# Down products one pass later and gathers indexed three passes ahead in the expert loop of a hybrid attention and MoE block

## The reference

```python
def _swiglu(x, wg, wu, wd):
    return (jax.nn.silu(x @ wg) * (x @ wu)) @ wd

def _moe(h, w_r, b_r, wg, wu, wd, swg, swu, swd):
    idx, wts = _route(h, w_r, b_r)
    return _moe_routed(h, idx, wts, wg, wu, wd) + _swiglu(h, swg, swu, swd)
```

## Time and profile before

| | |
|---|---|
| median of 3 runs | 3259.84 us |
| profiled execution, span | 3254.0 us; its own time about the median: 5.84 us lie around the span |
| expert loop of layer 0, first gate/up to last down products | 918.3 to 1796.6 us, 64 passes |
| expert loop of layer 1 | 2519.3 to 3213.1 us, 48 passes |
| TensorE busy, whole span | 2721.8 us (84%) |
| gate/up matmuls (L1402) | 806.1 us busy |
| down matmuls (L1414) | 417.5 us busy |

### The profile page before, as it was taken

The page is one execution under the profiler, slowest core; times in us unless marked ns, Lnnn a source line. Parts: engine busy times, 40 slices in busy tenths (PEclk is TensorE's granted clock), DMA queues, the critical chain, the costliest instruction groups (busy, mean ns, idle before and its releaser), DMA issues. The chain is left out here.

```text
span 3254.0 us, 44151 instructions
## 1 busy us (share of the span) xinstructions
PE 2721.8 (84%) x12983; PEld 1458.1 (45%) x12984; DVE 1251.3 (38%) x3394; ACT 562.2 (17%) x1256; POOL 1085.5 (33%) x948
## 2 busy tenths in 40 slices
PE   6688988996969999999989368899977888889884
PEld 5364755654533333333333146666743333333331
DVE  5653553433323333333333564453533323323223
ACT  2121321311001111111111212321310111111111
POOL 0675798901011111111111273767410111111111
PEclk9898999997989999999999689899987999999997
DMA  6120212114187998999896411122134999998983
GB/s 225 33 75 26 87 56 93 49 40 161 58 314 228 330 303 262 298 304 300 293 333 212 166 33 55 33 85 89 53 109 172 339 391 370 386 386 261 367 331 110
DMA packets 193069, 635.88 MB, mean 195 GB/s; under 512 B 18768, under 2 KB 113232, under 8 KB 159440
## 3 DMA queue, kind: packets, MB, share of 16 engines
q1 hardware_dynamic: 159856, 530.30, 43.4%
q0 software_dynamic: 33120, 104.37, 14.0%
HBM read 577.72 MB, written 76.94 MB: 201 GB/s over the span
## 5 line engine op out<-in xcount | busy, mean ns | idle before, releaser
L1402 PE MATMUL ps<-wgu,xT 128*64 128x512 f32 x3584 | 806.1, 602 | 82.9 <-issue 65.4
L1402 PEld LDWEIGHTS ps<-wgu,xT 128*64 128x64 f32 x3584 | 297.7, 138 | 588.9 <-issue 588.9
L1342 POOL DMA_INDIRECT X<-h_rows,gix x116 | 119.0, 1026 | 1070.5 <-DVE wc L1520 1024.9
L1414 PE MATMUL ps<-wd,hiddenT 128*64 128x512 f32 x1792 | 417.5, 605 | 37.1 <-issue 35.5
L544 PE MATMUL ps<-w_in,hT 128*128 128x512 f32 (+3 forms) x1152 | 395.6, 504 | 16.2 <-DMA wup_1B<-in_w_up 4.4
L544 PEld LDWEIGHTS ps<-w_in,hT 128*128 128x128 f32 x1152 | 212.4, 202 | 184.7 <-issue 177.0
L1361 POOL DMA_INDIRECT ffn_rows<-Y,six x112 | 179.0, 1598 | 252.2 <-issue 221.6
L1414 PEld LDWEIGHTS ps<-wd,hiddenT 128*64 128x64 f32 x1792 | 148.3, 139 | 234.8 <-issue 227.5
L1530 DVE TENSOR_TENSOR hidden<-silu,ps 128x256 f32<-128x256 f32 x112 | 47.2, 421 | 395.0 <-ACT silu L1477 395.0
L1389 PE MATMUL ps<-cst,X 128*128 128x128 f32 x912 | 147.3, 286 | 56.0 <-DMA X<-h_rows,gix 55.4
L1477 ACT ACTIVATE silu<-ps 128x256 f32<-128x256 f32 x112 | 42.9, 383 | 807.8 <-PE ps L1402 807.8
(11 more groups left out here) (453 smaller groups left out, 3716.0 us busy)
## 6 DMA issues: line engine op xcount, KB each, us to landing
wgu<-in_exp_gu SPq DMA_DIRECT2D x128, 2048.0 KB, 11.9
wd<-in_exp_d SPq DMA_DIRECT2D x128, 1024.0 KB, 10.3
ada_start<-in_ada_w SPq DMA_DIRECT2D x8, 1024.0 KB, 9.9
w_in<-in_w_in SPq DMA_DIRECT2D x4, 2048.0 KB, 8.2
w_in<-in_w_out SPq DMA_DIRECT2D x4, 2048.0 KB, 11.2
aw_0A<-in_ada_w SPq DMA_DIRECT2D x12, 512.0 KB, 4.0
aw_0B<-in_ada_w SPq DMA_DIRECT2D x12, 512.0 KB, 3.8
w_in<-in_w_in SPq DMA_DIRECT2D x2, 3072.0 KB, 10.7
```

What stands on the lines that cost most here:

```text
L1342: pool.indirect_dma_start(out=X[j][:, :], out_offset=None, in_=v.h2_dram, in_offset=bass.IndirectOffsetOnAxis(ap=gix[j][:, 0:1], axis=0), ...
L1402: last = pe.matmul(ps[h * HB:(h + 1) * HB, 0, :], xT[:, k, h * HB:(h + 1) * HB], wgu[w[h]][:, k, :], start=(k == 0), stop=(k == KD - 1))
L1414: last = pe.matmul(ps[h * HB:(h + 1) * HB, 1 + c, :], G[:, f, h * HB:(h + 1) * HB], wd[w[h]][:, f, c * 512:(c + 1) * 512], start=(f == 0), ...
```

## The change: what it does

In the changed code, TensorE's pass i turns all eight blocks of pass i + 1, then does the down products of pass **i - 1**, turns the hidden rows of pass i, makes the list of pass i + 3, and does the gate/up products of pass **i + 1** at its end. Gate/up of pass 0 stands before the loop, the down products of the last pass behind it; in pass 0 down products are done on zeros. It reads six table entries at its start: three of pass i - 1 and three of pass i + 1. The other engines follow: Y of pass i - 1 is written in pass i, gathers fetch pass i + 3 after the scatter, lists and marks are three ahead, the row numbers are kept in a tile of one column per pass. SyncE loads gate/up of expert e, then down of expert e - 1.

```diff
...
+                with sp.Fori(0, E // NB - 2) as group:
                     for w in range(NB):
-                        e = group * NB + w
-                        free = sp.value_load(table[0:1, bass.ds(e + T_FREE, 1)], min_val=0, max_val=pairs)
-
-                        sp.wait_ge(gate_up, free + GU_CREDIT)
-                        sp.dma_start(wgu[w][:, :, :].rearrange("p k n -> p (k n)"),
-                                     v.t["exp_gu"][l][bass.ds(e, 1)].rearrange("a p n -> (a p) n")).then_inc(w_gu[w], 16)
-                        sp.wait_ge(down, free + DOWN_CREDIT)
-                        sp.dma_start(wd[w][:, :, :].rearrange("p k n -> p (k n)"),
-                                     v.t["exp_d"][l][bass.ds(e, 1)].rearrange("a p n -> (a p) n")).then_inc(w_d[w], 16)
+                        e = group * NB + (NB + 1 + w)
+                        load_gate_up((w + 1) % NB, e, free_after(e))
+                        load_down(w, e - 1, free_after(e - 1))
...
-                def body(i, turn, j):
-                    pool.wait_ge(index, i + 3)
-                    pool.wait_ge(turned_b, i + 1)
-                    pool.wait_ge(wcol, i * 2 + 2)
-                    waited()
-                    gather(j)
+                def scatter(j):
+                    pool.sem_inc(y_free, 1)
+                    pool.indirect_dma_start(out=v.acc_dram, out_offset=bass.IndirectOffsetOnAxis(ap=six[j][:, 0:1], axis=0),
+                                            in_=Y[j][:, :], in_offset=None, compute_op=ALU.add).then_inc(added, 16)
+
+                def body(i, j):
+                    before = 1 - j
                     pool.wait_ge(y_act, i + (1 + CREDIT))
                     pool.wait_ge(y_dve, i + (1 + CREDIT))
                     pool.wait_ge(y_index, i + 1)
                     pool.wait_ge(added, i * 16 + 16)
-                    pool.sem_inc(y_free, 1)
-                    pool.indirect_dma_start(out=v.acc_dram, out_offset=bass.IndirectOffsetOnAxis(ap=six[j][:, 0:1], axis=0),
-                                            in_=Y[j][:, :], in_offset=None, compute_op=ALU.add).then_inc(added, 16)
-
+                    scatter(before)
+                    pool.wait_ge(index, i + (AHEAD + 1))
+                    pool.wait_ge(turned_b, i + 2)
+                    pool.wait_ge(wcol, i * 2 + 6)
+                    waited()
+                    gather(before)
...
+                def turn_rows(j):
+                    for k in range(KD):
+                        last = pe.transpose(ps[:, 3 + k // 4, k % 4 * P:(k % 4 + 1) * P], X[j][:, k * P:(k + 1) * P], v.ident)
+                        if k == 3:
+                            last.then_inc(turned_a, 1)
+                    last.then_inc(turned_b, 1)
...
-                def body(i, turn, odd):
-                    variant = entry(pe, T_VAR, i, 2 * NB - 1)
-                    landed = [entry(pe, T_LAND0 + h * TABN, i, E // NB * 16) for h in range(2)]
-                    pe.wait_ge(x_act, i + 1)
-                    pe.wait_ge(x_dve, i + 1)
-                    pe.wait_ge(hidden, i + CREDIT)
-                    by_buffers(variant, gate_up_products, landed, 0, 2 * NB)
-                    pe.wait_ge(index, i + 2)
-                    token_list(i + 2)
+                def entries(i):
+                    return entry(pe, T_VAR, i, 2 * NB - 1), [entry(pe, T_LAND0 + h * TABN, i, E // NB * 16) for h in range(2)]
+
+                def body(i, turn, odd, turns16):
+                    was, was_landed = entries(i - 1)
+                    now, now_landed = entries(i + 1)
                     with pe.If(odd < 1):
                         pe.wait_ge(gathered[1], turn * 16 + 16)
-                        turn_rows(1, 0)
+                        turn_rows(1)
                     with pe.Else():
                         pe.wait_ge(gathered[0], turn * 16 + 32)
-                        turn_rows(0, 0)
+                        turn_rows(0)
+                    pe.wait_ge(g_act, i + CREDIT)
+                    pe.wait_ge(g_dve, i + CREDIT)
+                    pe.wait_ge(y_act, i + CREDIT)
+                    pe.wait_ge(y_dve, i + CREDIT)
+                    by_buffers(was, down_products, was_landed, 0, 2 * NB)
                     pe.wait_ge(hidden, i + (1 + CREDIT))
                     turn_hidden()
-                    with pe.If(odd < 1):
-                        turn_rows(1, 1)
-                    with pe.Else():
-                        turn_rows(0, 1)
-                    pe.wait_ge(y_act, i + CREDIT)
-                    pe.wait_ge(y_dve, i + CREDIT)
-                    by_buffers(variant, down_products, [*landed, i + 1], 0, 2 * NB)
-
-                token_list(0)
-                pe.wait_ge(index, 1)
-                token_list(1)
+                    pe.wait_ge(index, i + AHEAD)
+                    pe.wait_ge(listed, i + (AHEAD + 1))
+                    token_list()
+                    with pe.If(i * 8 + 8 < turns16):
+                        pe.wait_ge(x_act, i + 2)
+                        pe.wait_ge(x_dve, i + 2)
+                        by_buffers(now, gate_up_products, now_landed, 0, 2 * NB)
+
+                for b in range(AHEAD):
+                    if b:
+                        pe.wait_ge(index, b)
+                    pe.wait_ge(listed, b + 1)
+                    token_list()
                 pe.wait_ge(gathered[0], 16)
-                turn_rows(0, 0)
-                turn_rows(0, 1)
+                turn_rows(0)
                 total = pe.value_load(table[0:1, T_COUNT:T_COUNT + 1], min_val=0, max_val=pairs)
+                turns16 = passes16(pe)
+                first, landed = entries(0)
+                pe.wait_ge(hidden, CREDIT)
+                pe.wait_ge(x_act, 1)
+                pe.wait_ge(x_dve, 1)
+                by_buffers(first, gate_up_products, landed, 0, 2)
                 with pe.Fori(0, -(-turns // STRETCH)) as stretch:
                     with pe.If(stretch * (STRETCH * U) < total):
                         with pe.Fori(0, STRETCH) as k:
                             turn = pe.snap(stretch * STRETCH + k)
                             with pe.If(turn * U < total):
                                 with pe.Fori(0, U) as odd:
-                                    body(pe.snap(turn * U + odd), turn, odd)
+                                    body(pe.snap(turn * U + odd), turn, odd, turns16)
+                last, landed = entries(turns16 // 8 - 1)
+                pe.wait_ge(g_act, turns16 // 8 + CREDIT)
+                pe.wait_ge(g_dve, turns16 // 8 + CREDIT)
+                pe.wait_ge(y_act, turns16 // 8 + CREDIT)
+                pe.wait_ge(y_dve, turns16 // 8 + CREDIT)
+                by_buffers(last, down_products, landed, 0, 2 * NB)
 
+                def row_index(i, j):
+
+                    dve.wait_ge(y_free, i + 1)
+                    dve.tensor_scalar(six[j][:, :], rows[:, bass.ds(i, 1)], cst[:, C_ADD:C_ADD + 1], None, ALU.add).then_inc(y_index, 1)
+
+                def y_half(i, j):
+
+                    dve.wait_ge(down, i + 1)
+                    dve.wait_ge(wcol, i * 2 + 2)
+                    dve.tensor_scalar(Y[j][:, 512:D], ps[:, 2, :], wc[j][:, 0:1], None, ALU.mult).then_inc(y_dve, 1)
+
+                def body(i, j):
+                    before = 1 - j
+                    e1, e3 = entries(i + 1), entries(i + AHEAD)
                     dve.wait_ge(silu, i + 1)
                     dve.tensor_tensor(HID[:, :], SG[:, :], ps[:, 0, FD:2 * FD], ALU.mult).then_inc(hidden, 1)
+                    x_half(i + 1)
+                    dve.wait_ge(indexed, i + AHEAD)
+                    mark_slots(i + AHEAD, e3, i * 4 + (4 * AHEAD + 2))
+                    row_index(i, before)
+                    y_half(i, before)
                     dve.wait_ge(g_turned, i + 1)
-                    dve.wait_ge(down, i + DOWN_CREDIT)
                     dve.tensor_copy(G[:, 1, :], ps[:, 7, 0:P]).then_inc(g_dve, 1)
-                    x_half(i + 1)
-                    dve.wait_ge(y_free, i + 1)
-                    dve.tensor_scalar(six[j][:, :], gix[j][:, :], cst[:, C_HALF:C_HALF + 1], None, ALU.add).then_inc(y_index, 1)
-                    dve.wait_ge(y_index, i + 1)
-                    dve.wait_ge(gathered[j], turn * 16 + 16)
-                    dve.wait_ge(indexed, i + 3)
-                    make_index(j, i * 4 + 11)
-                    dve.wait_ge(y_act, i + CREDIT)
-                    dve.wait_ge(y_dve, i + CREDIT)
-                    weight_column(e1, (j + 1) % U)
-                    dve.wait_ge(down, i + (1 + DOWN_CREDIT))
-                    dve.wait_ge(wcol, i * 2 + 2)
-                    dve.tensor_scalar(Y[j][:, 512:D], ps[:, 2, :], wc[j][:, 0:1], None, ALU.mult).then_inc(y_dve, 1)
-
...
```

More of the change, by code:

```diff
@@ L1300, in experts @@
         mark = sb("mark", [P, nt, P], F16)
-        itmp = sb("itmp", [P, 3])
+        itmp = sb("itmp", [P, 2])
+        rows = sb("rows", [P, TABN])
```

(50 more changed lines are left out.)

80 lines of the change are left out of this document (49 added, 31 removed).

## The result

The changed kernel takes 3455.19 us (median of 4 runs, 3451.25 to 3458.4) against 3259.84: 1.0603 times the time before, 95% interval 1.0589 to 1.0617. I had forecast 3297, and a range up to 3325. The profiled execution has a span of 3456.4 us against 3254.0, so +202.4 (more than the 195 between the medians, since the profiled execution of after is one of its two longer ones).

| stretch | before | after | more | forecast |
|---|---|---|---|---|
| from the first to the second gate/up | 15.2 / 15.2 | 18.5 / 19.1 | 7.2 | 0 |
| layer 0, 62 passes | 850.2 | 979.8 | 129.6 | 14 |
| layer 1, 46 passes | 665.7 | 694.9 | 29.2 | 3 |
| last gate/up to the end of the last down products | 12.9 / 12.9 | 29.0 / 23.7 | 26.9 | 21 |
| all outside the loops | | | 9.4 | 0 |

A forecast was written before the change was run, and what follows sets the result against it. Transfers and TensorE were both taken as bounds, with "issue" the largest single idle item in layer 0. Layer 0 +14, layer 1 +3 and ends +21 gave +38 on the 3259.84 us median: 3297 us, range 3242 to 3325.

The forecast's parts named there:

- my first rival: TensorE's queue covers the whole gate/up, so the 1.38 us idle a pass vanish: 3182 us; 5%.
- six entries 5 x 0.76 + 0.65 = 4.45: Sequencer behind the gate/up products: six table reads take 4.45 us of a 5.25 or 5.9 us walk.
- 0.09 for clock falls as before: Layer 0 pass: clock falls add 0.09 us, unchanged, to 13.81, giving 13.90 against 13.71.
- The 13.9 us pass: Sign in the profile after: a layer 0 pass takes 13.9 us.
- Transposes to down products, 0.13: Between the eight transposes and the down products, 0.13 us a pass of sequencer work stays uncovered.
- Down to gate/up 0: From down products through hidden transposes and list to gate/up: no idle time, or up to 0.3 us if it slips.
- Gathers' waits end: Gathers are issued 18 us ahead of use instead of 9.3, so their waits end in both layers.
- Layer 1, +3: Layer 1's loop: no gain because DMA engines are full over more than half; +3 us, bounds -18 and +20.
- Ends, +21: Last down products, moved behind each loop's exit, start late: +11.7 and +9.2 us, together +21, bounds 8 and 28.
- the seam is shorter: Sequencer's walk overlaps what was added in a row, 0.5 us a pass less: 3256 or 3246 us; 15%.
- the list comes late: VectorE's marks slip beyond the 0.3 us in hand, TensorE waits each pass: +34 us, 3331 us; 9%.
- SP starves layer 1: SP's new order starts loads 6 us later and empties DMA queues, 15 to 20 us: 3315 us; 11%.

The follow-up runs named there:

- late_reads: Changed kernel with the three table entries for the gate/up products read behind the down products, not behind the gate/up products; 3197.86 us, 0.9812 of before.
- packed: Changed kernel with variant and both landed counts in one table word, so TensorE reads 2 words a pass instead of 6; 3176.71 us, 0.9745 of before.
- before_six: Kernel before the change, with three more table entries read and not used at the start of each TensorE pass; 3584.14 us, 1.0995 of before.
- small_write: Changed kernel with the scatter replaced by a plain write of 16 columns of Y to fixed rows (layer 1 works on other data); 3290.85 us, 1.0107 of before.
- filled: Changed kernel with one useless 64x384 matmul behind each of the six table reads and the waits for Y ahead of them; 3528.93 us, 1.0813 of before.
- gather_first: Changed kernel with GpSimd issuing the gather ahead of the scatter in each pass; 3446.39 us, 1.0558 of before.
- plain_write: Changed kernel with the scatter replaced by a plain write of the whole of Y to fixed rows (layer 1 works on other data); 3356.88 us, one run.
- packed_late_scatter: Changed kernel with one packed table word per entry set (2 reads a pass) and layer 0's scatter issued behind those reads; 3255.81 us, 0.9977 of before.
- packed_plus2: Changed kernel with packed table words and two more unused table reads at each pass's start, 4 in all; 3267.56 us, 1.0027 of before.

## Why the prediction was wrong

- *The mechanism held.* The sequencer's walk behind the gate/up products sets the seam; late_reads and packed show it by taking it away, before_six by lengthening the old one. In the timeline's first pass the loop's ALU_OP stands at 1149.14, 2.88 us behind gate/up's start, so the cover from there is 4.21 us (I had 4.24), and the walk from there to the transposes at 1156.23 is 7.09: my 5.9 and 1.19 by which one read is held. The Trainium skill (TensorE: Matmul & The Clock Gate, the table at its head) gives the queue a depth of 64. If all 64 records of a gate/up stood in it, the cover would be the whole 7.09, as in my first rival; the runs disagree again, with the sequencer held for 2.6 us at the full clock.
- *Step that failed: "six entries 5 x 0.76 + 0.65 = 4.45".* It took the price of a read from places where no read had met the scatter. 57 reads held by 0.99 us are 56 us of the 65 by which layer 0's idle time exceeds my 1.51 x 62 = 93.6. With no read held (small_write), the seam is 1.49 against 1.38. I had named a pass over 14.1 as the sign that a wait I called covered is open; the pass is 15.80, and no such wait is: the six reads themselves are longer.
- *Second step that failed: "0.09 for clock falls as before".* I took the number of stretches from a kernel with 1.26 us idle a pass and let it stand for one with more, in one piece. At 2.56 there are 38, and the products behind cost 48.8 us more in layer 0 and 8.7 in layer 1. Without held reads, small_write has 6: the first error brought most of the second. The Trainium skill (the same page, "A second HAM failure mode: psum-queue depth-cycling") says that a TensorE that idles between groups of matmuls can make its clock swing; the trace agrees, with 38 stretches at 1.2 GHz at 2.56 us idle a pass and none in filled; I had left it out.
- *The 13.9 us pass* would have been right but for these two terms: small_write has 14.00. That its whole time (3290.85) lies near the 3297 is luck in part: layer 1 works on other data there.
- *Transposes to down products, 0.13:* measured 5.3 / 62 = 0.09 (6.9 / 62 = 0.11 in small_write). *Down to gate/up 0:* right, 0.6 us in 62 passes. *Gathers' waits end:* right, none in either stretch. The list was in time.
- *Layer 1, +3:* measured +29.2, of it 20.5 idle and 8.7 busy. Waits for weights are 21.3, against 17.2 before: SP's new order did not starve it by the 15 to 20 us of the rival. Its seam is 1.75, not 1.38, with 13 long reads; that transfers would hide the longer seam there was wrong: late_reads took 52 us off the same 46 passes.
- *Ends, +21:* measured 26.9. The wait ahead of layer 0's last down products was 7.78, I had 6.7; and they then ran mostly at the halved clock, 6.52 us instead of 3.65, which I had not priced. (The terms that the prediction names for these starts add to 10.3 and 7.7, not to its 10.7 and 8.2; the 1 us changes nothing.) First passes (+7.2) and the stretches outside (+9.4) I had at nothing; their causes were not tried.

```profile
1942.66 6.52 PE L1442 MATMUL ps<-wd,hiddenT 128*64 128x512 f32 x16 [7.78 <-issue]
```

- *Rivals.* "The queue covers the whole gate/up", "the seam is shorter", "the list comes late", "SP starves layer 1" and "no effect" are all refuted. What happened, a longer seam that also costs clock, was on no list.

## What to carry to other kernels

Reorder a loop only after asking what its sequencer does at the new seam: here the same reorder lost 195 us with six table reads behind the gate/up products and gained 83 with two. Price scalar work at the seam in the place where it will stand, beside the transfers that will run then, and add the slow clock of what follows when the array stands idle for long in one piece. If a table entry has three small numbers, pack them.

## What the runs showed of the hardware

- Table reads of an engine (0.30 us) can be held, TensorE's to 1.3 us on average and up to 1.6 (gather_first), when they fall some 0.5 to 2.5 us behind the end of GpSimd's issue of a 512 KB write: TensorE's, VectorE's and SyncE's alike. With 8 KB written none was held, and with the 512 KB moved later neither TensorE's nor VectorE's were.
- What in the write holds a read stays open. At this distance 98% of the held reads of the changed kernel's layer 0 have 8 or more of the write's 4096-byte packets in flight 0.6 us after their start, and 6% of the others; in plain_write it is 15% and 18%. Nor is it shown why so few are held in layer 1. The load of the DMA engines alone is not it: packed has a share of 0.95 in layer 0 with 48 long reads of 124, and 0.96 in layer 1 with 3 of 92.
- Half-clock stretches do not follow mean idle time alone: packed_late_scatter has 13 at 1.04 us a pass, packed_plus2 3 at 1.27. The traces show how differently the idle time is spread: 14 single pieces of 2 us or more in the first, 11 of them with half clock in them or up to 6 us behind, and one such piece in the second. In the changed kernel it is so for 22 of the 23 pieces of 2.8 us or more, and for 2 of the 11 between 1.2 and 2.
